# A two-layer decoder trunk on one core: the expert-retrieval queries as token-by-feature products of 512 weight columns, copied and transposed back

## What is computed

```python
q = (hf @ w_q).astype(jnp.float32).reshape(t_, PEER_HEADS, 2, PEER_QHALF)   # 1024 -> 8 heads x 2 x 128
scores = jnp.einsum('thpd,hpnd->thpn', q, subkeys.astype(jnp.float32))     # against 128 keys
top_s, top_i = lax.top_k(scores, PEER_TOPK)                                # 16 of each half
...
u_sel = u_tab[ii]                                  # 8 heads x 16 experts a token, 1024 numbers each
act = jax.nn.gelu(jnp.einsum('td,tkd->tk', xi, u_sel), approximate=False)
return jnp.einsum('tk,tkd->td', w, v_tab[ii])      # and 1024 numbers each of a second table
```

## Time and profile before

| | |
|---|---|
| median of 3 runs | 1617.02 us (1616.6 to 1618.84) |
| the profiled execution: its own time | 1618.45 us |
| span of its trace | 1616.7 us |
| TensorE busy | 1435.8 us, 89%; 4450 products and 4450 weight loads recorded |
| VectorE, ScalarE, GpSimd busy | 980.3, 667.3, 651.9 us (61, 41, 40%) |
| DMA | 629.72 MB, of it 536.90 MB gathered rows and 91.60 MB in the hardware queue |
| granted TensorE clock, mean | 0.987 |
| chain that ended last | 40% TensorE, 38% DMA, 10% VectorE, 4% ScalarE |

### The profile page before, as it was taken

The page is one execution under the profiler, slowest core; times in us unless marked ns, Lnnn a source line. Parts: engine busy times, 40 slices in busy tenths (PEclk is TensorE's granted clock), DMA queues, the critical chain, the costliest instruction groups (busy, mean ns, idle before and its releaser), DMA issues.

```text
span 1616.7 us, 14850 instructions
## 1 busy us (share of the span) xinstructions
PE 1435.8 (89%) x4450; PEld 705.7 (44%) x4450; DVE 980.3 (61%) x2487; ACT 667.3 (41%) x1841; POOL 651.9 (40%) x535
## 2 busy tenths in 40 slices
PE   7999989999867989898887999899989889797786
PEld 6646445555423434343352545355335344342222
DVE  1226578758758766743356855566456777777654
ACT  1514544544534435332243433343344454544434
POOL 1002334555434333233345334333334544556672
PEclk9999999999999999999999999999999999999999
DMA  5443999999999999999999999999999999999995
GB/s 211 156 156 134 422 419 421 421 422 421 421 422 421 421 422 421 421 422 421 421 422 421 398 422 421 422 421 415 422 422 412 422 420 422 422 421 422 421 421 217
DMA packets 87088, 629.72 MB, mean 390 GB/s; under 512 B 9808, under 2 KB 9952, under 8 KB 10720
## 3 DMA queue, kind: packets, MB, share of 16 engines
q0 software_dynamic: 73728, 536.90, 80.0%
q1 hardware_dynamic: 13104, 91.60, 13.9%
q10 hardware_dynamic: 176, 0.28, 0.1%
HBM read 627.69 MB, written 1.05 MB: 389 GB/s over the span
## 4 chain that ended last, share of the span: by engine, by line
PE 40%; DMA 38%; DVE 10%; ACT 4%; issue 4%; POOL 3%; SPq 0%; POOLq 0%; DVEq 0%; ACTq 0%
DMA ring<-in_peer_uv,experts 37%; PE acc L1569 21%; PE work L1339 6%; DVE ring L1218 5%; PE work L1356 5%; POOL ring L675 3%; PE work L1328 3%; PE acc L1532 1%; ACT diag L867 1%; PE work L1423 1%; ACT gelus L865 1%; PE work L1371 1%; DMA weights<-in_c_w_in 1%; DMA weights<-in_ab_w_in 1%; PE work L1284 1%
## 5 line engine op out<-in xcount | busy, mean ns | idle before, releaser
L1569 PE MATMUL acc<-ring,diag 128*128 128x512 f32 x2048 | 979.4, 611 | 156.9 <-ACT diag L867 155.6
L675 POOL DMA_INDIRECT ring<-in_peer_uv,experts x512 | 642.4, 1255 | 848.0 <-PE acc L1569 700.9
L1218 DVE CUSTOM_DVE_ANT_0 ring<-ring,h 128x1024 f32<-128x1024 f32 x512 | 624.2, 1227 | 431.4 <-DMA ring<-in_peer_uv,experts 423.3
L1569 PEld LDWEIGHTS acc<-ring,diag 128*128 128x128 f32 x2048 | 367.3, 191 | 687.6 <-ACT diag L867 351.1
L864 ACT ACTIVATE gelus<-dots 128x1 f32<-128x1 f32 x512 | 103.0, 201 | 677.6 <-DVE dots L1218 676.8
L867 ACT ACTIVATE diag<-ident,gelus 128x128 f32<-128x128 f32 x512 | 205.6, 402 | 16.7
L865 ACT ACTIVATE gelus<-gelus,gates 128x1 f32<-128x1 f32 x512 | 150.8, 294 | 16.6
L1339 PE MATMUL work<-weights,hT 128*128 128x512 f32 x288 | 135.0, 599 | 5.6 <-DMA weights<-in_c_w_in 5.6
L1356 PEld LDWEIGHTS work<-hT,weights 128*128 128x128 f32 x704 | 86.2, 192 | 21.0 <-issue 21.0
L1356 PE MATMUL work<-hT,weights 128*128 128x128 f32 x704 | 87.0, 275 | 0.0
L1339 PEld LDWEIGHTS work<-weights,hT 128*128 128x128 f32 x288 | 54.8, 192 | 72.2 <-issue 65.7
(11 more groups left out here) (198 smaller groups left out, 839.5 us busy)
## 6 DMA issues: line engine op xcount, KB each, us to landing
weights<-in_c_w_in SPq DMA_DIRECT2D x25, 1024.0 KB, 9.9
weights<-in_peer_w_q SPq DMA_DIRECT2D x14, 1024.0 KB, 9.6
weights<-in_ab_w_in SPq DMA_DIRECT2D x10, 1024.0 KB, 7.2
ring<-in_peer_uv,experts POOLq DMA_INDIRECT x512, 19.8
weights<-in_c_w_out SPq DMA_DIRECT2D x6, 1024.0 KB, 9.9
z<-in_c_w_out SPq DMA_DIRECT2D x6, 1024.0 KB, 11.1
z<-in_peer_w_q SPq DMA_DIRECT2D x5, 1024.0 KB, 9.2
weights<-in_ab_w_out SPq DMA_DIRECT2D x4, 1024.0 KB, 7.1
```

Source lines behind the costliest of these rows:

```text
L675: pool.indirect_dma_start(ring[:, t % SLOTS, :], None, uv_rows, bass.IndirectOffsetOnAxis(ap=experts[:, b, step:step + 1], axis=0))\
L1218: nc.vector.tensor_tensor_reduce(out=ring[:, k, 0:D], in0=ring[:, k, 0:D], in1=h[:, b, :], scale=1.0, scalar=0.0, op0=ALU.mult, op1=ALU.ad ...
L1569: last = nc.tensor.matmul(acc[2 * b + n][:, :], diag[:, k, :], ring[:, k, D + n * CH:D + (n + 1) * CH], start=False, stop=True, skip_group ...
```

## The change

The 15 products of four tiles are turned round. New stages QTALL and QWIDE (four pieces, `Q_PIECES`) use `tall`: the tokens are the stationary operand, and 512 columns of weights stream past (8 products, 2 a piece). That gives token by feature, so QCOPY copies the bank to `queries` (ScalarE), QTURN transposes it in four transposes into a new work bank (TensorE), QBACK copies that back over it (ScalarE), and QDOT goes on as before. Behind the last piece QCOPY stands one step, QTURN two, QBACK three, QDOT four (before: two), DTAKE five (before: four). In several places `ranked` starts one step later. A piece needs one half of the chunk alone, and for a chunk's last user `tall` counts `half_used` after the second piece, for which SP waits before it reloads the first half. The early products of one head stay as they were. Shortened:

```diff
 def projected(at, layer, b, m, gap=2):
     q = (layer, b, m, ALL)
-    steps = [int(at + gap * i) for i in range(TILES)]
+    steps = [int(at + gap * i) for i in range(Q_PIECES)]
     done = steps[-1] + 1
-    return ([(steps[0], ("QPROD", *q))] + [(steps[i], ("QMORE", *q, i)) for i in range(1, TILES)]
-            + [(done, ("QTAKE", *q)), (done + 1, ("QDOT", *q)), (done + 3, ("DTAKE", *q))])
+    return ([(steps[0], ("QTALL", *q))] + [(steps[i], ("QWIDE", *q, i)) for i in range(1, Q_PIECES)]
+            + [(done, ("QCOPY", *q)), (done + 1, ("QTURN", *q)), (done + 2, ("QBACK", *q)), (done + 3, ("QDOT", *q)),
+               (done + 4, ("DTAKE", *q))])
...
-                for i, k in enumerate((2, 3, 0)):
-                    out += mixed(int(at) + 2 + 2 * i, b, k)
+                for wait, k in ((2, 2), (3, 3), (9, 0)):
+                    out += mixed(int(at) + wait, b, k)
...
-    return sorted(out + projected(at + 5, 1, b, 0, 1.5) + ranked(at + 14, 1, b, 0), key=lambda entry: entry[0])
+    return sorted(out + projected(at + 5, 1, b, 0, 1.5) + ranked(at + 15, 1, b, 0), key=lambda entry: entry[0])
...
-            + ranked(39, 1, b, 4, 2) + ranked(52, 1, b, 5, 2) + ranked(68, 1, b, 6, 2) + ranked(83, 1, b, 7, 2))
+            + ranked(39, 1, b, 4, 2) + ranked(52, 1, b, 5, 2) + ranked(69, 1, b, 6, 2) + ranked(83, 1, b, 7, 2))
...
-    return (out + projected(12, 0, 0, 1, 1) + ranked(20, 0, 0, 2) + ranked(26, 0, 0, 3)
-            + projected(27, 0, 0, 2) + ranked(38, 0, 0, 4, 2) + projected(38, 0, 1, 1, 5) + ranked(50, 0, 0, 5, 2)
-            + projected(56, 0, 1, 2, 3) + projected(68, 0, 0, 3, 1.5) + ranked(77, 0, 0, 6) + projected(76, 0, 1, 0, 4)
+    return (out + projected(12, 0, 0, 1, 1) + ranked(21, 0, 0, 2) + ranked(27, 0, 0, 3)
+            + projected(27, 0, 0, 2) + ranked(39, 0, 0, 4, 2) + projected(38, 0, 1, 1, 5) + ranked(50, 0, 0, 5, 2)
+            + projected(56, 0, 1, 2, 3) + projected(68, 0, 0, 3, 1.5) + ranked(78, 0, 0, 6) + projected(76, 0, 1, 0, 4)
...
-    if kind == "QPROD":
+    if kind == "QTALL":
         last = (0, 1, *args[2:]) if args[0] == 0 else args
-        done = places["QMORE", *last, TILES - 1] if len(args[3]) == PHEADS else places["QTAKE", *args]
-        return (done, done)
+        return (places["QWIDE", *last, 1], places["QWIDE", *last, 3])
...
+def last_use(layer, b, m):
+    return layer == 1 or (b == 1 and m > 0)
...
-                    if layer == 1:
-                        load_chunk(chunk, peer_w_q[layer, m], 2 * [filled(bank)], b)
-                    elif b == 0:
-                        load_chunk(chunk, peer_w_q[layer, m], 2 * [filled(BANKS["QPROD", layer, 1, m, heads])])
+                    if layer == 1 or b == 0:
+                        last = (layer, b if layer else 1, m, heads)
+                        load_chunk(chunk, peer_w_q[layer, m], [(half_used, HALVES["QWIDE", *last, 1]), filled(BANKS["QTALL", *last])], b)
...
+                elif kind in ("QCOPY", "QBACK"):
+                    w = await_bank(act, bank)
+                    nc.scalar.activation(queries[:, QUERIES[*args,], :], w[:, :], ACT.Copy).then_inc(free[bank % WB], 1)
...
+                elif kind in ("QTALL", "QWIDE"):
+                    layer, b, m, heads, q = *args[:4], args[4] if kind == "QWIDE" else 0
+                    tall(bank, None if first_chunk_holds(layer, m) else chunk, hT, b, q, Q_PIECES, last_use(layer, b, m))
+                elif kind == "QTURN":
+                    own_copies(BANKS["QTALL", *args], 1)
+                    fill_transposed(bank, queries[:, QUERIES[*args,], :])
```

More of the change, by code:

```diff
@@ L50, in banks_of @@
             "VEC": lambda: 2, "VVEC": lambda: 2,
-            "QPROD": lambda: 1, "QDOT": lambda: 1,
+            "QPROD": lambda: 1, "QTALL": lambda: 1, "QTURN": lambda: 1, "QDOT": lambda: 1,
             "ZPROJ": lambda: 1, "MIXG": lambda: 1, "MIXT": lambda: 1, "MIXO": lambda: 1,
             }.get(kind, lambda: 0)()
-TAKES = {"HTAKE": "TRANSPOSE", "STAKE": "SOUT", "GLATAKE": "GLAT", "QTAKE": "QPROD", "DTAKE": "QDOT", "QMORE": "QPROD", "ZMORE": "ZPROJ", "OMORE": "MIXO",
+TAKES = {"HTAKE": "TRANSPOSE", "STAKE": "SOUT", "GLATAKE": "GLAT", "QTAKE": "QPROD", "DTAKE": "QDOT", "QMORE": "QPROD", "QWIDE": "QTALL", "QCOPY": "QTALL", "QBACK": "QTURN", "ZMORE": "ZPROJ", "OMORE": "MIXO",
          "ZTAKE": "ZPROJ", "GTAKE": "MIXG", "TTAKE": "MIXT", "OTAKE": "MIXO"}
-PIECES_OF = {"QMORE": 4, "ZMORE": 2, "OMORE": 2}
+PIECES_OF = {"QMORE": 4, "QWIDE": 4, "ZMORE": 2, "OMORE": 2}
 def first_chunk_holds(layer, m):
@@ L89 @@
 TILES = 2 * PHEADS
+Q_PIECES = 4
 Z_PIECES = 4
@@ L184, in trunk_for @@
             out += projected(at, 1, *between[j], gap)
-            at += gap * TILES
+            at += gap * Q_PIECES
     for n in range(2):
@@ L263, in walk @@
         if first == (kind, *args):
-            shared = kind == "QPROD" and args[0] == 0 and args[1] == 1 and args[2] > 0
-            chunks[first] = chunks["QPROD", 0, 0, *args[2:]] if shared else chunk
+            shared = kind == "QTALL" and args[0] == 0 and args[1] == 1 and args[2] > 0
+            chunks[first] = chunks["QTALL", 0, 0, *args[2:]] if shared else chunk
         yield kind, args, Place(banks[kind, *args], chunks.get(first, chunk), x_writes, banks)
@@ L341 @@
 for _stage in PLAN:
-    if (_stage[0] == "ZMORE" and _stage[3] == 1) or (_stage[0] == "OMORE" and _stage[3] in (1, 3, 5)):
+    if (_stage[0] == "ZMORE" and _stage[3] == 1) or (_stage[0] == "QWIDE" and _stage[5] == 1 and last_use(*_stage[1:4])) or (_stage[0] == "OMORE" and _stage[3] in (1, 3, 5)):
         HALVES[_stage] = len(HALVES) + 1
@@ L349 @@
     BANKS[_kind, *_args] = _at.bank
-    if _kind == "QPROD":
+    if _kind in ("QPROD", "QTALL"):
         QUERIES[*_args,] = len(QUERIES) % 3
@@ L588, in _ @@
                     sp.dma_start(keysT[:, :, :], peer_keys[args[0]]).then_inc(keys_in, 16)
-                elif kind == "QPROD" and not first_chunk_holds(args[0], args[2]):
+                elif kind == "QTALL" and not first_chunk_holds(args[0], args[2]):
                     layer, b, m, heads = args
-                    if layer == 1:
-                        load_chunk(chunk, peer_w_q[layer, m], 2 * [filled(bank)], b)
-                    elif b == 0:
-                        load_chunk(chunk, peer_w_q[layer, m], 2 * [filled(BANKS["QPROD", layer, 1, m, heads])])
+                    if layer == 1 or b == 0:
+                        last = (layer, b if layer else 1, m, heads)
+                        load_chunk(chunk, peer_w_q[layer, m], [(half_used, HALVES["QWIDE", *last, 1]), filled(BANKS["QTALL", *last])], b)
                 elif kind == "ZPROJ":
@@ L1331, in wide, with tall @@
                         last.then_inc(full[(n + i // per) % WB], 1)
-            def tall(n, chunk, src, b, q=0, pieces=1):
+            def tall(n, chunk, src, b, q=0, pieces=1, releases=True):
                 ks = range(q * KT // pieces, (q + 1) * KT // pieces)
-                wt = await_chunk(pe, chunk, sorted({k // 4 for k in ks}))
+                if chunk is None:
+                    pe.wait_ge(first_chunk_in, 16)
+                    wt = [first_chunk[:, k, :] for k in range(KT)]
+                else:
+                    wt = await_chunk(pe, chunk, sorted({k // 4 for k in ks}))
                 w = work[n % WB] if q else claim_bank(pe, n)
@@ L1342, in tall, with query_tile @@
                     last.then_inc(full[n % WB], 1)
-                elif q == pieces // 2 - 1:
+                elif q == pieces // 2 - 1 and releases:
                     last.then_inc(half_used, 1)
-            def query_tile(n, chunk, layer, b, m, heads, i=0):
-                if first_chunk_holds(layer, m):
-                    pe.wait_ge(first_chunk_in, 16)
-                    wt = [first_chunk[:, k, :] for k in range(KT)]
-                else:
-                    wt = await_chunk(pe, chunk)
+            def query_tile(n, layer, b, m, heads, i=0):
+                pe.wait_ge(first_chunk_in, 16)
+                wt = [first_chunk[:, k, :] for k in range(KT)]
                 w = work[n % WB] if i else claim_bank(pe, n)
@@ L1541, in _ @@
                 elif kind == "QPROD":
-                    query_tile(bank, chunk, *args)
+                    query_tile(bank, *args)
                 elif kind == "QMORE":
-                    query_tile(bank, chunk, *args)
+                    query_tile(bank, *args)
+                elif kind in ("QTALL", "QWIDE"):
[4 more added lines that the diff above has]
+                    fill_transposed(bank, queries[:, QUERIES[*args,], :])
                 elif kind == "QDOT":
@@ L1547, in _ @@
                     pe.wait_ge(keys_in, 16 * (layer + 1))
-                    own_copies(BANKS["QPROD", *args], 1)
+                    own_copies(BANKS["QTURN" if len(heads) == PHEADS else "QPROD", *args], 1)
                     w = claim_bank(pe, bank)
```

6 lines of the change are left out of this document (3 added, 3 removed).

## The result

The changed kernel takes **1622.09 us** (median of 12 runs, 1620.46 to 1623.85), the kernel before beside it 1618.84 us (12 runs, 1616.59 to 1620.06). The ratio is 1.0023, with an interval of 1.0015 to 1.0032: slower by 2.4 to 5.2 us. The forecast was 1618.5 and the range ended at 1621.6. It stood on the median of 3 runs of the kernel before, 1617.02; 12 runs gave 1618.84. The rival "the dry queue costs more" is the one that came true: its loss of 3.6 us fits the ratio, and its 1620.6 is low because it stood on the same 1617.0.

What follows compares the result with a forecast made beforehand. Transfers, paced by one late DMA engine, were taken as the bound; products, copies, banks and halves 0, later scores +1.5 on a median of 1617.0 gave 1618.5 us, own range 1616.0 to 1620.2, wider range 1615.8 to 1621.6.

Steps and rivals of the forecast that it cites:

- the dry queue costs more: Rival: at 237 to 241 us the pacing engine has run dry and loses the full 3.6 us; 1620.6 us, chance 0.20.
- What bounds it: Whole kernel: transfers set the pace from about 150 us, and one late DMA engine works on alone at the end.
- The products: TensorE: pieces save 0.28 us a product, four transposes cost 0.44; 2.4 us over 15, nothing at the end.
- The copies: ScalarE: one more copy a product, 0.60 us each, 9 us in all, covered by gathers in flight; 0.
- The banks: One more bank a product; the tightest claim, MIXT of group 3, is covered by 1.72 us of gather products; 0.
- The freed halves: Weight loads on SP: earlier loads gain 0; layer 1 keys and halves move from 439.38 to about 445 us, covered.
- The later scores: Layer 0, block 0, head 2: scores 3.6 us later, GpSimd's issue near 237 us delayed; +1.5 us, bounds 1.3 and 3.6.
- Fewer instructions to fetch: Rival: 660 fewer products, so 5.2 fewer packets in queue 8; -5.4 us if its engine paced, 1611.6 us, chance 0.04.
- Nothing in layer 1: Later blocks: rankings end before they are asked for, cost nothing; a second wait for experts in layer 1 would refute the forecast.

Runs made afterwards that it cites:

- apart_sooner: Changed kernel with the pieces of product (0, 0, 1) from step 10 instead of 12, ranking at 20 and 26 as before the change; 1619.10 us, ratio 1.0004.
- first_old: Changed kernel with product (0, 0, 1) and the ranking behind it made the old way, the other 14 products still turned; 1617.28 us, ratio 0.9999.
- no_release: Changed kernel with both halves of a query chunk freed only after the last piece, as in the kernel before; 1622.35 us, ratio 1.0029.
- late_scores: Kernel before, no product turned, with QDOT of product (0, 0, 1) two steps later, its DTAKE and ranking one step later; 1620.62 us, ratio 1.0017.
- sooner1: Changed kernel with the pieces of product (0, 0, 1) and the ranking behind it one step sooner; 1620.08 us, ratio 1.0009.
- close_turn: Changed kernel; for product (0, 0, 1) copy, transposes and copy back on one step, QDOT and ranking at their old steps; 1619.57 us, ratio 1.0012.
- later_scores: Kernel before with QDOT of product (0, 0, 1) four steps later, DTAKE one step behind it, ranking three steps later; 1624.23 us.

## Why the prediction failed, step by step

- **What bounds it: right.** Transfers from 150 us on, one late engine with some 10 us alone at the end.
- **The products: right.** +0.16 us each, 2.4 in all, by forecast. Piece 1.72 and transposes 0.44 us came as computed. The sum of busy time can't show it: 1435.8 us before and 1438.6 after, but 1434.6 in apart_sooner, which has the same instructions as the change. first_old and apart_sooner show no cost at the end. By an estimate from the spacing of 131 ns that the Trainium skill gives for 512 columns (TensorE: Matmul & The Clock Gate, Back-to-back issue gap) a piece would last 0.52 us; the trace of the change has 1.72 again, so for these float32 products the rows decide.
- **The copies: right.** 30 copies of 595 ns for 15 of 598: 8.8 us for 9, covered.
- **The banks: right.** No wait of a product for a bank shows in TensorE's waits.
- **The freed halves: right at the end, wrong on the way.** They are worth nothing that shows (no_release). But the keys of layer 1 were issued at 453.88 us (439.01 before) and the halves behind them at 454.25, not at 445: QDOT in front of them came at 452.80 after 437.93, 14.9 us later, of which some 5 are the whole stream's and 5 the two steps; what made the rest was not looked into. The first use behind it, at 531.49, had room for all of it: the one wait of such a product for c_w_in is 5.5 us, as before.
- **The later scores: this step failed, in its last line.** The delay was right: from the stage ahead of the product (201.24 and 203.09 us) to QDOT (219.78 and 225.31) it is 18.54 us before and 22.22 after, 3.7 for the forecast 3.6. The place and the wait (about 11 forecast, 10.56 seen) were right too. What failed is "I take +1.5, near the lower end": the runs show 3.7 us (2.4 to 5.2 by the ratio). I had priced the loss by the landing of the last engine, +1.3, as if the engine that paces the end still had work in hand in this stretch. It did not: between 242 and 244 us the share is 0.00, so all sixteen stood still, the late one too. late_scores, sooner1, close_turn and later_scores show that the loss follows the delay. The sentence before it had the right reason and I did not follow it: the late engine "got so late only afterwards", so at 240 us it had no backlog to live on. That last part is argued. No view names the engine that ends last, and the full standstill is 2 us, less than the 3.7 lost; in late_scores the share does not fall below 0.15 in two microseconds, and the loss is still 2.7. The term is mis-sized: 1.5 for 3.7, where the upper bound of the prediction, 3.6, was nearly right.
- **Fewer instructions to fetch: the packets right, the gain rightly refused.** Queue 8 went from 35 to 30 and bought nothing: first_old and apart_sooner fetch less of TensorE's program and are not faster. In these runs it is queue 14 that counts.
- **Nothing in layer 1: right.** No wait for experts behind 700 us is longer than 1 us. One that I had not named stands in block 1 of layer 0, 10.84 us at 683.77, where the kernel before had at most 3.88 in those 200 us. The transfers stay at 421 and 422 GB/s over it, so it cost them nothing, where the same wait at 240 us was followed by a dip. Only this trace has it: no_release, sooner1 and apart_sooner have none over 3.9 us there, so it belongs to the execution as much as to the change.

The term is half of the miss. The medians of 12 runs are 3.3 us apart for the 1.5 forecast, which is 1.8 of the 3.6 us by which 1618.5 is off. The other 1.8 is the base: I put the difference on 1617.0, the median of 3 runs, though the profiled execution of 1618.45 stood 1.4 above it, and 12 runs gave 1618.84. With the term at 3.6 on that base the sum is 1620.6, still 1.5 under the measured time. And with both bounds known (1.3 and 3.6 us) and a share of 0.93 that said that engines were already dry, the two should have had about even chances.

What stays open: the profiled execution of the change is 1.6 us late already at 203 us, before the turned product ran (A is 5.2 later and the product explains 3.7). late_scores has 0.8 us of the same kind, and no_release against first_old has none (95.5 and 91.8, 3.7 apart). I take it for the difference between executions; no run was made to show it. Open too are which engine paces at 240 us and why sooner1 pays so little for its dip.

## What to carry to other kernels

Where a full stream of transfers is the bound, look for the one place where its queue is nearly dry (the longest wait of the issuing engine with the transfers just below their ceiling), and price a delay there near its full length. Elsewhere a wait of the same length can pass without a dip, as the 10.84 us at 683.77 did. A change that adds latency but hardly any work then costs only where it moves that one stage, and starting this stage sooner takes the cost away. But start it no sooner than its inputs can be there: here the engine that ranks also makes the products that come before a slot is free, and while it waits for scores it does neither. And take the base of a forecast from more than 3 runs where they lie some 2 us apart.

## What I had not expected of the hardware

- Where a kernel starts sets a part of its spread. In the profiled executions the first gather issue falls between 143.9 and 146.7 us, and the time from there to the last expert does not follow it (no_release starts at 143.85 and the change at 146.42, with B 1 us apart), which is why B tells kernels apart better than spans do. In the first 12 runs of the kernel before the times stand in two groups, 1616.6 to 1617.3 and 1618.8 to 1620.1; the 29 runs of the next series fill the gap between them.
